# Dummy products of the identity in the second attention and in the routing of a two-layer decoder step

## What is computed

```python
# layer 0: block-sparse attention, then a dense SwiGLU of 2816
x = x + moba(rope(rmsnorm(q)), rope(rmsnorm(k)), v) @ w_o_a
x = x + swiglu(rmsnorm(x), w_gu_dense, w_down_dense)
# layer 1: three dilation groups over shared keys and values, merged by their denominators
x = x + merge([dilated(q_g, k, v) for g in ((128, 1), (512, 4), (2048, 16))]) @ w_o_b
# then the top 2 of 8 SwiGLU experts of 3584, by a router
logits = rmsnorm(x) @ w_router
x = x + sum(gate_e * swiglu_e(rmsnorm(x)) for e in top2(logits))
```

## Time and profile before

| what | value |
|---|---|
| median of three runs | 1415.11 us (1414.82 to 1417.55) |
| span of the profiled execution | 1420.3 us; nothing else of that execution's time is recorded |
| PE busy | 1398.1 us, 98% of the span |
| mean granted clock of TensorE | 0.995 of full |
| second attention in the profile | from 456 to 505 us |
| its output projection | from 505 to 521 us |
| router, routing and gather | from 521 to 537 us |
| the eight experts | from 537 to 1417 us |

### The profile page before, as it was taken

One profiled execution on the slowest core, in us unless ns is written; L12 is line 12 of the kernel. 1 busy time (PEld: TensorE's weight loads), 2 busy tenths in 40 slices (PEclk: granted clock), 3 DMA queues, 4 the chain that ended last, 5 costly groups with the idle time before them and its releaser, 6 DMA issues.

```text
span 1420.3 us, 35327 instructions
## 1 busy us (share of the span) xinstructions
PE 1398.1 (98%) x16009; PEld 1014.8 (71%) x16009; DVE 451.1 (32%) x954; ACT 327.5 (23%) x635; POOL 180.1 (13%) x222
## 2 busy tenths in 40 slices
PE   9999999999999889999999999999999999999998
PEld 7885999999998573774674675675575575575475
DVE  7867666664587531120120120120120120120121
ACT  6446644433553643001001001001001001001000
POOL 5723320000175621000000000000000000000100
PEclk9999999999999989999999999999999999999999
DMA  8958795535745277999999999999999999999993
GB/s 269 319 169 312 248 360 177 162 106 169 261 159 213 71 313 302 386 418 420 408 417 420 409 418 420 408 419 420 407 418 419 407 419 419 410 418 420 397 419 154
DMA packets 146427, 471.62 MB, mean 332 GB/s; under 512 B 9760, under 2 KB 81824, under 8 KB 117472
## 3 DMA queue, kind: packets, MB, share of 16 engines
q1 hardware_dynamic: 138544, 439.48, 79.4%
q0 software_dynamic: 7728, 29.82, 5.8%
HBM read 451.17 MB, written 18.09 MB: 330 GB/s over the span
## 4 chain that ended last, share of the span: by engine, by line
PE 95%; DVE 2%; ACT 1%; issue 1%; DMA 1%; SPq 0%; DVEq 0%; ACTq 0%
PE psum L1197 41%; PE psum L1237 20%; PE psum L350 9%; PE psum L351 9%; PE psum L352 9%; PE psum L909 1%; PE psum L845 1%; PE psum L970 1%; PE psum L931 1%; PE psum L894 1%; PE psum L949 1%; DMA raw<-in_w_qkv_a 1%; PE psum L1181 0%; PE psum L836 0%; DVE wlo L346 0%
## 5 line engine op out<-in xcount | busy, mean ns | idle before, releaser
L1197 PE MATMUL psum<-wexp,xg 128*32 128x512 f32 (+1 forms) x6144 | 588.3, 539 | 0.2
L1197 PEld LDWEIGHTS psum<-wexp,xg 128*32 128x32 f32 x6144 | 339.9, 110 | 239.3 <-issue 201.9
L1237 PE MATMUL psum<-wexp,act 128*32 128x256 f32 x5376 | 298.1, 379 | 0.0
L1237 PEld LDWEIGHTS psum<-wexp,act 128*32 128x32 f32 x5376 | 207.2, 109 | 86.4 <-issue 0.2
L2003 DVE TENSOR_TENSOR am<-sg,psum 128x512 f32<-128x512 f32 (+1 forms) x48 | 26.9, 617 | 736.3 <-issue 486.7
L350 PE MATMUL psum<-hh,whi 128*128 128x288 f32 x696 | 207.4, 298 | 0.0
L351 PE MATMUL psum<-hl,whi 128*128 128x288 f32 x696 | 205.3, 295 | 0.0
L352 PE MATMUL psum<-hh,wlo 128*128 128x288 f32 x696 | 205.1, 295 | 0.0
L346 DVE TENSOR_TENSOR wlo<-raw,whi 128x2048 fp32r<-128x2048 f32 (+1 forms) x66 | 144.0, 2181 | 54.7 <-ACT whi L342 54.7
L350 PEld LDWEIGHTS psum<-hh,whi 128*128 128x128 f32 x696 | 130.8, 188 | 8.5 <-issue 8.3
L351 PEld LDWEIGHTS psum<-hl,whi 128*128 128x128 f32 x696 | 130.9, 188 | 0.1
(11 more groups left out here) (301 smaller groups left out, 1066.0 us busy)
## 6 DMA issues: line engine op xcount, KB each, us to landing
wexp<-in_w_moe SPq DMA_DIRECT2D x224, 1024.0 KB, 12.0
wexp<-in_w_moe SPq DMA_DIRECT2D x128, 768.0 KB, 10.5
raw<-in_w_gu_dense SPq DMA_DIRECT2D x22, 1024.0 KB, 6.5
wexp<-in_w_moe SPq DMA_DIRECT2D x32, 512.0 KB, 11.3
raw<-in_w_qkv_a SPq DMA_DIRECT2D x12, 1024.0 KB, 10.6
raw<-in_w_down_dense SPq DMA_DIRECT2D x16, 704.0 KB, 4.6
raw<-in_w_q_b SPq DMA_DIRECT2D x6, 1024.0 KB, 6.0
h_rows<-zeros POOLq DMA_DIRECT2D x14, 384.0 KB, 10.1
```

What stands on the lines that cost most here:

```text
L1197: ins = nc.tensor.matmul(ps[NG * part + r][32 * j:32 * j + 32, 0:wd], xg[:, r, 32 * k:32 * k + 32], wexp[:, q % RING, wd * j:wd * j + wd], ...
L1237: ins = nc.tensor.matmul(ps[6 + r // 2][32 * j:32 * j + 32, 256 * (r % 2):256 * (r % 2) + 256], act[:, r, 32 * kk:32 * kk + 32], wexp[:, q ...
```

## The change

TensorE's program gets a helper that issues n float32 products of the identity with itself into a piece of PSUM that nobody reads afterwards, and calls it in six places: three products in step t = 2 of the second attention; twice three in each of the steps t = 7, 8 and 9 (t > n with n = 6 units); and 2, 3 and 1 in the routing. Three of the places also get a wait: for all four value tiles to be turned (`vtok_done`), for all scores to be masked (`masked`), and for ScalarE's row norms (`column_ready`). Nothing else is changed.

```diff
+            def idle_products(out, n):
+
+                for i in range(n):
+                    nc.tensor.matmul(out, con("ident"), con("ident"), start=True, stop=True)
+
...
                     kind1, i1 = unit_at(b, t - lag)
+                    if ng > 1 and t == 2:
+                        eng.wait_ge(sem(f"vtok_done_{tg}"), nj)
+                        idle_products(pv_out(b, 0)[:, 0:P], 3)
+                    if ng > 1 and t > n:
+                        eng.wait_ge(sem(f"masked_{tg}"), scored_count(b, len(b["jobs"]) - 1))
+                        idle_products(ps[b["score_banks"][0]][:, 0:P], 3)
                     for k in jobs_of(b, t - lag)[0:1]:
                         turn_probs(k, kind1)
...
                     if kind3 == S_:
                         pick_rows(i3)
+                    if ng > 1 and t > n:
+                        idle_products(ps[b["score_banks"][0]][:, 0:P], 3)
                     for k in jobs_of(b, t - lag)[1:2]:
                         turn_probs(k, kind1)
...
             for i in range(2, 6):
                 turn_gained(i)
 
+            eng.wait_ge(sem("column_ready"), 1)
+            idle_products(ps[5][:, 256:384], 2)
             eng.wait_ge(sem("chosen"), 1)
...
             ins.then_inc(sem("placed"), 1)
+            idle_products(ps[5][:, 256:384], 3)
             turn_raw(0)
             turn_raw(1)
+            idle_products(ps[5][:, 256:384], 1)
```

## The result

The change makes the kernel slower: 1420.10 us median of 15 runs (1417.32 up; one run of 2913.25 us, never seen again, is left out of the comparison) against 1416.31 us (1414.44 to 1419.43) of the kernel before, also of 15 runs. The ratio, the measure of all comparisons here, is 1.0019, 95% interval 1.0011 to 1.0028, so +2.7 us where +0.5 was forecast; the two medians lie 3.8 us apart. Of the 4.5 us between the forecast time and the measured one, 1.2 is the start: the forecast added to 1415.11, the median of three of these runs of the kernel before, and all 15 give 1416.31. Run again later beside other kernels it was 1419.62 against 1416.96 us, 1.0023 (1.0013 to 1.0033).

What follows compares the result with a forecast made beforehand. TensorE, busy 1398.1 of 1420.3 us, was taken to bound the kernel. Terms 0.6 + 0.2 - 0.8 = 0.0 us, plus 0.5 for other executions, on 1415.11 gave 1415.6 us, range 1413.2 to 1418.8.

Steps and rivals of the forecast that it cites:

- Step t = 2: Second attention: three dummies ahead of transposes that waited for nothing delay the sample scores, +0.6 us (0.1 to 0.7).
- One dummy: Cost of a float32 identity product: two passes of 0.123 us each, bounds 0.059 and 0.142.
- Rival C: All dummies: cheap at 0.059 us a pass, the parts together -2.55 us, 1412.6 us; chance 0.10.
- Steps t = 7 to 9: Before the output projection: what the full clock saves, the dummies spend, +0.2 us (-1.4 to +0.7).
- rival A: Last steps: dummies are pure cost; second branch, no clock fall there anyway, +3.1 us; overall 1418.9 us, chance 0.18.
- The routing: Routing: gather starts 0.7 us later but saves 1.5 at full clock, together -0.8 us (-1.25 to -0.6).
- rival B: Routing: gather stays at half clock, routing +0.7 to +1.2 us, 1416.9 us in all; chance 0.20.
- The sum and its +0.5 for other executions: Whole kernel: parts sum to 0.0 us; +0.5 added for one run in three without the half-clock gather.
- The expert stage follows its start: Expert stage: length stays 880 us, so any shift of its first products moves the end by the same amount.

Runs made afterwards that it cites:

- before again: The kernel before, unchanged, run once more as a control with a second profile: 1418.09 against 1417.19 us, 1.0006.
- change again: The whole change run again beside other kernels, against the kernel before: 1419.62 against 1416.96 us, 1.0023.
- no nine: Only the nine dummies of t = 7 and 8 before the last values, none between those and the projection, against the kernel before: 1416.14 against 1417.19 us, 0.9995.
- pauses (again): Repeat of the version with dummies only in TensorE's pauses, none ahead of ready work, against the kernel before: 1414.04 against 1416.96 us, 0.9982.

## Why the prediction was wrong

The stages of the profiles, in us, each as the distance of two starts or of an end and a start in the timeline; an asterisk marks half clock in part of the stage:

| stage | before | before again | change | change again | no nine | pauses (again) |
|---|---|---|---|---|---|---|
| first sample scores to second | 12.06* | 12.06* | 10.94 | 10.94 | 10.36 | 10.37 |
| end of the last sample values to the last pair's values | 6.32* | 5.96 | 7.99* | 6.61 | 6.61 | 5.96 |
| from there to the projection | 1.48* | 0.80 | 2.83 | 2.83 | 0.80 | 0.80 |
| the projection | 15.39* | 13.79 | 13.76 | 13.76 | 13.79 | 13.79 |
| places counted to the gather's end | 6.89* | 6.80* | 7.73* | 7.73* | 5.42 | 5.42 |

- **Step t = 2, +0.6: right.** 10.94 against 10.36 at full clock, 0.58.
- **One dummy, 0.123 us a pass: near enough.** 0.113 in the row of 18, 0.128 in the six of t = 2 (0.77 over six). Rival C, at 0.059, is out. The 0.123 divided the transposes' row by its length to the modelled end; by the distance of starts 16 of them take 1.81 us (525.26 to 527.07 in the changed kernel), 0.113, just what a dummy in a row costs.
- **Steps t = 7 to 9, +0.2: this step failed.** It set the dummies against a projection whose first 15 products run at half clock, as the earlier trace rows have it. That half clock is not a property of the kernel: its second profile has none of it. At full clock in both, the three stages come to 23.20 with the change and 20.55 without, +2.65; the second branch of rival A said +3.1. Even against the first profile's slow projection (23.19) the changed one's 24.58 is +1.4, since the 2.19 us pause stays open and the clock was down from about 500.3, some 0.4 us behind the first dummy's start, to 503.6.
- **The routing, -0.8: failed.** It is rival B: the gather stays at half clock in part in both profiles of the change, and the stage is 0.8 to 0.9 longer than in the two of before. The profile with the routing's six dummies alone has 7.72, half clock in part again. And the gather also runs at full clock, in 4.22 us, without any routing dummy: in the profiles with and without the nine and in the one with the last pauses filled. So the 1.5 us that the forecast credited to the six dummies comes and goes by itself. (What the prediction calls 18 products of eight columns are nine products in 18 passes; nothing hangs on it.)
- **The sum and its +0.5 for other executions: the wrong way to weigh them.** The path is 0.58 + 2.65 + 0.9 = 4.1 us longer where the clock behaves alike. What comes back is the clock: over the runs of one comparison its mean rose from 0.9961 (35 runs) to 0.9971 (12 runs), and (1 - 0.9961) x 1415 - (1 - 0.9971) x 1418 = 1.4 us of TensorE's time. 4.1 - 1.4 = 2.7, an estimate; the means of the same runs lie 3.0 apart, with an interval of 1.8 to 4.7 by the ratio. The estimate leaves out the kernel's end: from TensorE's last product to the end of the span it is 5.0 and 6.2 us in the change's two profiles and 4.25 in both of before; and half clock in that time (0.50 from 1416.4 to 1418.8 in the second profile of the change, with no product left) costs nothing though it counts in the mean. Whether this end belongs to the change is open. The forecast took the clock's part at its largest, from one execution with three half-clock stretches, and put the dummies' own time against that.
- **The expert stage follows its start: right for TensorE.** From its first to its last product it takes 875.2 us in every profile but the first (878.8). What differs is the end behind it, 4.2 to 6.2 us, in which the last outputs are stored: so the whole stage is 879.5 to 881.5 us, and with a spread of 2 us there, one profile's span cannot price a loss of 2.7.

That dummies in the pauses of the last steps raise the clock and shorten the time is shown: with all pauses filled the mean clock is 0.9988 over 12 runs against 0.9961, with the last steps' pauses alone 0.9982 and with the first one alone 0.9963. That the open pauses are what pulls the clock down is not shown. None of the three profiles that fill the last pauses has half clock between 496 us and the projection's end, but of the eleven others four have none there either, two of them of the kernel before and of the change themselves; and the nine dummies that leave the 2.19 us pause open gave a mean clock of 0.9977. How far the two dummies before the places help the gather is open: of those three profiles one has it at 5.65 us with them, two at 4.22, one of these without them.

## What to carry to other kernels

A dummy product belongs into a pause that TensorE has anyway, sized to leave a rest of it; put ahead of work that is ready, it costs its full time in every execution and returns the clock only in some. In the last steps the mean clock rose from 0.996 to 0.9973 with the eighteen, to 0.9977 with the nine before the last values, to 0.9982 with the twelve in the pauses, but only to 0.9963 with the nine in front of the projection. Their time on the path was 2.65, 0.65, 0 and 2.0 us at full clock. Which of the three pauses matters was not tried one by one. Before a stretch at half clock is counted as a gain, take a second profile: where it comes and goes, the gain is its mean over executions and not what one of them shows.

## What the runs showed of the hardware

The clock differs from execution to execution of the same kernel, and the time follows it: of the 35 runs of the kernel before in the last comparison, the 15 with a mean clock of 0.995 have a span of 1416.2 us on average and the 4 with 0.999 one of 1412.6. These 3.6 us are more than half of the spread of its times (1413.40 to 1419.92), and more than the change itself.
